# First product and gelu of 64 of 128 expert tiles computed beside the top-k routing and kept in device memory

## What is computed

```python
def _peer(x, w_q, sub_keys, u_tab, v_tab):
    q = (xt @ w_q).reshape(T, PEER_HEADS, 2, PEER_DK // 2)
    s = jnp.einsum('thpd,hpkd->thpk', q, sub_keys)
    s1, i1 = lax.top_k(s[:, :, 0], PEER_TOPK)
    s2, i2 = lax.top_k(s[:, :, 1], PEER_TOPK)
    cand_s = s1[..., :, None] + s2[..., None, :]          # all pairs
    top_s, pos = lax.top_k(cand_s, PEER_TOPK)
    gate = jax.nn.softmax(top_s, axis=-1)
    hid = jnp.einsum('td,thkd->thk', xb, u_tab[ib])       # first product
    coef = jax.nn.gelu(hid, approximate=False) * gb
    return jnp.einsum('thk,thkd->td', coef, v_tab[ib])    # second product
```

## Time and profile before

| | us |
|---|---|
| median of 3 runs (2864.67 to 2868.19) | 2864.67 |
| the profiled execution | 2865.48 |
| its span in the trace | 2863.7 |
| of it `peer_route` (DVE's first to last operation) | 107.7 |
| of it `peer_table` | 107.4 |
| of it the expert stream, first matmul to last | 721.4 |

### The profile page before, as it was taken

The page is one execution under the profiler, slowest core; times in us unless marked ns, Lnnn a source line. Parts: engine busy times, 40 slices in busy tenths (PEclk is TensorE's granted clock), DMA queues, the critical chain, the costliest instruction groups (busy, mean ns, idle before and its releaser), DMA issues. The chain is left out here.

```text
span 2863.7 us, 43489 instructions
## 1 busy us (share of the span) xinstructions
PE 2196.3 (77%) x16766; PEld 1930.6 (67%) x16766; DVE 1775.3 (62%) x2988; ACT 903.8 (32%) x1244; POOL 113.3 (4%) x102
## 2 busy tenths in 40 slices
PE   4936665997844599679778876550679999999997
PEld 2936334996733599467476776550569999999996
DVE  2564226776775677467336668459976666666665
ACT  1300222432323233132322422220554444444443
POOL 0000000000000000043000023000000000000000
PEclk8955557999865799889765988785899999999998
DMA  5635005884702487231100000310025555555554
GB/s 184 221 59 151 0 2 183 320 310 171 258 10 76 160 299 281 74 119 59 59 3 1 5 3 27 138 59 0 0 95 185 183 189 190 184 183 190 189 183 148
DMA packets 153588, 368.84 MB, mean 129 GB/s; under 512 B 10992, under 2 KB 93680, under 8 KB 141296
## 3 DMA queue, kind: packets, MB, share of 16 engines
q1 hardware_dynamic: 153312, 365.93, 36.7%
q10 hardware_dynamic: 144, 1.05, 0.1%
HBM read 364.32 MB, written 2.62 MB: 128 GB/s over the span
## 5 line engine op out<-in xcount | busy, mean ns | idle before, releaser
L981 PE MATMUL experts_pa<-all_h_hi,experts_u_hi 128*128 128x256 f32 x1024 | 290.1, 283 | 7.4 <-DVE experts_u_lo L1052 7.4
L983 PE MATMUL experts_pa<-all_h_hi,experts_u_lo 128*128 128x256 f32 x1024 | 290.5, 284 | 0.0
L982 PE MATMUL experts_pa<-all_h_lo,experts_u_hi 128*128 128x256 f32 x1024 | 290.5, 284 | 0.0
L1228 PE MATMUL ffn_pa<-all_h_hi,ffn_u_hi 128*128 128x256 f32 x704 | 198.6, 282 | 29.6 <-DVE ffn_u_lo L1287 29.6
L1057 DVE TENSOR_TENSOR experts_v_lo<-experts_v,experts_v_hi 128x1024 fp32r<-128x1024 f32 x128 | 156.8, 1225 | 92.1 <-ACT experts_v_hi L1026 92.1
L981 PEld LDWEIGHTS experts_pa<-all_h_hi,experts_u_hi 128*128 128x128 f32 x1024 | 196.9, 192 | 12.5 <-DVE experts_u_lo L1052 7.6
L994 PE MATMUL experts_py<-experts_v_lo,experts_c_hi 128*128 128x512 f32 x512 | 201.0, 393 | 0.0
L982 PEld LDWEIGHTS experts_pa<-all_h_lo,experts_u_hi 128*128 128x128 f32 x1024 | 196.9, 192 | 4.9
L993 PE MATMUL experts_py<-experts_v_hi,experts_c_hi 128*128 128x512 f32 x512 | 200.1, 391 | 0.0
L1229 PE MATMUL ffn_pa<-all_h_lo,ffn_u_hi 128*128 128x256 f32 x704 | 198.1, 281 | 0.0
L1230 PE MATMUL ffn_pa<-all_h_hi,ffn_u_lo 128*128 128x256 f32 x704 | 197.9, 281 | 0.0
(11 more groups left out here) (543 smaller groups left out, 5467.5 us busy)
## 6 DMA issues: line engine op xcount, KB each, us to landing
experts_u<-in_peer_u SPq DMA_DIRECT2D x128, 512.0 KB, 4.4
experts_v<-in_peer_v SPq DMA_DIRECT2D x128, 512.0 KB, 3.3
ffn_u<-in_ffn_columns SPq DMA_DIRECT2D x44, 1024.0 KB, 7.9
ffn_ada_w<-in_ada_w SPq DMA_DIRECT2D x36, 1024.0 KB, 5.4
ffn_v<-in_ffn_rows SPq DMA_DIRECT2D x44, 512.0 KB, 8.1
proj_ada_w<-in_ada_w SPq DMA_DIRECT2D x12, 1024.0 KB, 5.7
proj_w<-in_diff_w_in SPq DMA_DIRECT2D x12, 1024.0 KB, 5.8
main_mod<-in_dn_w_qkv SPq DMA_DIRECT2D x24, 512.0 KB, 3.3
```

What stands on the lines that cost most here:

```text
L981: pe.matmul(out, u_hi[:, b, cols], h_hi[:, c, :], start=(c == 0), stop=False)
L982: pe.matmul(out, u_hi[:, b, cols], h_lo[:, c, :], start=False, stop=False)
L983: last = pe.matmul(out, u_lo[:, b, cols], h_hi[:, c, :], start=False, stop=(c == KT - 1))
L1228: pe.matmul(out, u_hi[:, b, cols], h_hi[:, c, :], start=(c == 0), stop=False)
```

## The change

`peer_route` gets a second job beside the routing: for tiles 0 to 63 it loads `u` (a ring of three buffers), splits it, multiplies it, applies gelu, and SP stores the result `hid` (128 x 256, 128 KB a tile) to a tensor `hid_kept` in device memory. On VectorE, `low_u` (the subtraction of one tile) is put between the groups of the top-16 search and of the `hot` steps. ScalarE does `high_u` two tiles ahead of the gelu; one `Exp` per token block stands between. SP's list holds loads and stores in turn. TensorE has the 64 products ahead of the six transposes.

`streamed_mlp` is replaced by `experts`, which is written out for all 128 tiles. For tiles 0 to 63 it loads `hid` (a ring of three) and `v`, and does only the weighing and `down`. For tiles 64 to 127 it does what was done before.

```diff
+        u = st.sb("u", [P, ring, D])
+        u_hi, u_lo = (st.sb(n, [P, ring, D], F32R) for n in ("u_hi", "u_lo"))
+        hid = st.sb("hid", [P, ring, S])
...
+        @block.sync
+        def _(sp):
+            for i in range(early + 2):
+                if i < early:
+                    if i >= ring:
+                        sp.wait_ge(u_split, i - ring + 1)
+                    sp.dma_start(u[:, i % ring, :], ins["peer_u"][i]).then_inc(u_loaded[i % ring], 16)
+                if i >= 2:
+                    sp.wait_ge(acted, i - 1)
+                    sp.dma_start(hid_kept[i - 2], hid[:, (i - 2) % ring, :]).then_inc(hid_kept_done[(i - 2) % ring], 16)
...
+            def low_u():
+                nonlocal tiles
+                if tiles < early:
+                    b = tiles % ring
+                    dve.wait_ge(u_hi_ready, tiles + 1)
+                    dve.tensor_tensor(u_lo[:, b, :], u[:, b, :], u_hi[:, b, :].bitcast(F32), ALU.subtract
+                                      ).then_inc(u_split, 1)
+                    tiles += 1
...
                 first = [done.at(dve.max(out_v[:, 0:8], values)) for values, out_v, _ in lists]
+                low_u()
...
                     rest.append(done.at(dve.match_replace(spare[n], out_v[:, 0:8], values, NEG)))
+                low_u()
...
                     second.append(done.at(dve.max(out_v[:, 8:16], spare[n])))
+                low_u()
...
+                    if n == 1 and values.shape[-1] > P:
+                        low_u()
+                low_u()
...
+            def high_u(i):
+                act.wait_ge(u_loaded[i % ring], 16 * (i // ring + 1))
+                if i >= ring:
+                    act.wait_ge(rows_ready, i - ring + 1)
+                act.copy(u_hi[:, i % ring, :], u[:, i % ring, :]).then_inc(u_hi_ready, 1)
+
+            def gate_tile(i):
+                act.wait_ge(rows_ready, i + 1)
+                if i >= ring:
+                    act.wait_ge(hid_kept_done[i % ring], 16 * (i // ring))
+                act.activation(hid[:, i % ring, :], pa[:, i % 2, 0:S], ACT.Gelu).then_inc(acted, 1)
+
+            high_u(0)
+            high_u(1)
+            for i in range(early):
+                if i + 2 < early:
+                    high_u(i + 2)
...
+                gate_tile(i)
...
+            for i in range(early):
+                b = i % ring
+                pe.wait_ge(u_split, i + 1)
+                if i >= 2:
+                    pe.wait_ge(acted, i - 1)
```

The stream in the changed kernel:

```diff
+            for i in range(n_tiles):
+                if i < early:
+                    if i >= ring:
+                        sp.wait_ge(weighed, i - ring + 1)
+                    sp.dma_start(hid[:, i % ring, :], hid_kept[i]).then_inc(hid_loaded[i % ring], 16)
+                if i >= 2:
                     sp.wait_ge(v_split, i - 1)
...
+                sp.dma_start(v[:, i % 2, :], rows[i]).then_inc(v_loaded[i % 2], 16)
+                j = i + 1 - early
+                if 0 <= j < late:
+                    if j >= 2:
+                        sp.wait_ge(u_split, j - 1)
+                    sp.dma_start(u[:, j % 2, :], columns[i + 1]).then_inc(u_loaded[j % 2], 16)
...
+            for i in range(n_tiles + 1):
+                if early <= i < n_tiles:
+                    up(i - early)
+                if i >= 1:
+                    down(i - 1)
...
+            high_v(0)
+            for i in range(n_tiles):
+                if i >= early:
+                    gate_tile(i - early)
+                if 0 <= i + 2 - early < late:
+                    high_u(i + 2 - early)
+                if i + 1 < n_tiles:
+                    high_v(i + 1)
...
+            low_v(0)
+            for i in range(n_tiles):
+                weigh(i)
+                if 0 <= i + 2 - early < late:
+                    low_u(i + 2 - early)
+                if i + 1 < n_tiles:
+                    low_v(i + 1)
```

More of the change, by code:

```diff
@@ L967, in _, with up @@
+            sp.wait_ge(u_split, late)
+            sp.dma_start(x, kept[0]).then_inc(x_loaded, 16)
             sp.wait_ge(v_split, n_tiles)
-            sp.dma_start(gate, kept[1]).then_inc(kept_loaded, 16)
+            sp.dma_start(gate, kept[1]).then_inc(gate_loaded, 16)
         @block.tensor
         def _(pe):
[L972 to L983, removed]
+            def up(j):
+                b = j % 2
+                pe.wait_ge(u_split, j + 1)
+                if j >= 2:
+                    pe.wait_ge(acted, j - 1)
+                out = pa[:, b, 0:S]
+                for c in range(KT):
+                    cols = slice(c * P, (c + 1) * P)
+                    pe.matmul(out, u_hi[:, b, cols], h_hi[:, c, :], start=(c == 0), stop=False)
+                    pe.matmul(out, u_hi[:, b, cols], h_lo[:, c, :], start=False, stop=False)
+                    last = pe.matmul(out, u_lo[:, b, cols], h_hi[:, c, :], start=False, stop=(c == KT - 1))
@@ L984, in up, with down @@
                 last.then_inc(rows_ready, 1)
-            def down(i, b, start=False, stop=False):
+            def down(i):
+                b = i % 2
+                start, stop = i == 0, i == n_tiles - 1
                 pe.wait_ge(coef_ready, i + 1)
@@ L1028, in gate_tile @@
[L1028 to L1058, removed]
+            def high_u(j):
+                act.wait_ge(u_loaded[j % 2], 16 * (j // 2 + 1))
+                if j >= 2:
+                    act.wait_ge(rows_ready, j - 1)
+                act.copy(u_hi[:, j % 2, :], u[:, j % 2, :]).then_inc(u_hi_ready, 1)
+            def high_v(i):
+                act.wait_ge(v_loaded[i % 2], 16 * (i // 2 + 1))
+                if i >= 2:
+                    act.wait_ge(down_done, i - 1)
+                act.copy(v_hi[:, i % 2, :], v[:, i % 2, :]).then_inc(v_hi_ready, 1)
@@ new lines, in low_v, with weigh @@
+            def low_v(i):
+                dve.wait_ge(v_hi_ready, i + 1)
+                dve.tensor_tensor(v_lo[:, i % 2, :], v[:, i % 2, :], v_hi[:, i % 2, :].bitcast(F32), ALU.subtract
+                                  ).then_inc(v_split, 1)
+            def weigh(i):
+                b = i % 2
+                if i < early:
+                    dve.wait_ge(hid_loaded[i % ring], 16 * (i // ring + 1))
+                    rows_of = hid[:, i % ring, :]
+                else:
+                    dve.wait_ge(acted, i - early + 1)
+                    rows_of = act_out[:, (i - early) % 2, :]
+                dve.tensor_tensor(coef[:], rows_of, table[:, i, :], ALU.mult).then_inc(weighed, 1)
```

134 lines of the change are left out of this document (63 added, 71 removed).

## The result

| | us |
|---|---|
| before, median of 4 runs beside the changed kernel | 2866.16 (2864.67 to 2868.19) |
| changed, median of 4 runs | 2971.60 (2969.18 to 2975.23) |
| ratio, 95% interval | 1.0368 [1.0350, 1.0386] |
| predicted | 2963, range 2920 to 3025 |
| span of the changed kernel's profiled execution | 2973.5 |

The change makes the kernel 3.7% slower. The busy time by stretch is read first again; it answers the earlier trace rows. The stretches are the routing, the first 64 tiles of the stream, the rest of it, and ten microseconds within the first 64. Columns: start:end, length, busy us and instructions of each engine, granted clock (PEclk), DMA share, GB/s.

The account below looks back on a forecast made before the run. It took VectorE to bound the routing and TensorE the stream before; after, one load in flight would pace the routing. 2865.48 + 242 - 144 = 2963.5, less 0.8 for the median: 2963 us, range 2920 to 3025.

Parts of the forecast that it names:

- The ring: Routing: load, rounding, gelu and store wait on each other, one load in flight; 5.4 us a tile, stage +242 us.
- The start and the end: Routing: fourth load issued at 12.2 us; after the last subtraction, 7.8 us remain to the last copy.
- The two `Exp` fall into waits: Routing, ScalarE: both operations fit into its waiting time, adding nothing to the 350 us stage.
- TensorE in the routing: Routing: busy half of the time; even a half-clock `up` of 5.1 us stays under 5.4 and costs nothing.
- The stream: First 64 tiles at 3.3 us each, the rest at 5.62; 583.5 us in place of 727.4, -144.
- The cold stream: Rival, 3%: TensorE at half clock in the stream's first 64 tiles, 5.3 us a tile, +128, total 3091 us.
- the joint: Stream, where tile 64 begins: `u(0)` loaded one tile late for ScalarE, 1 to 4 us, 3 taken.
- the lead: Stream start: first issue to first matmul takes 7.6 us, 6.0 before.
- Loads that run ahead: Rival, 6%: in the routing SP does not stand still at the stores; stage 201 us, total 2814 us.
- Later landings: Rival, 9%: in the routing store and load share the queue's rings; 6.3 to 6.6 us a round, 3017 to 3035.
- gain and cost would cancel: Rival, 1%: no change to be seen in the total, needing a routing round of 3.8 us.

Follow-up runs that it names:

- gelu first: Changed kernel with ScalarE doing the gelu of tile i ahead of the rounding of tile i+2, SP's list untouched: 2847.5 us (one run).
- 96 early tiles: Changed kernel with stores four tiles back, weighing ahead of `v_lo`, three `v` buffers, and 96 tiles moved in place of 64: 2784.23 us, 0.9721 of before.
- lag of four: Changed kernel with SP storing the `hid` of tile i-4 (in place of i-2) behind the load of tile i, five `hid` buffers: 2812.61 us, 0.9812 of before.

## Why the prediction held

**The ring.** It was the step that decided, and it held in detail: a round of 5.4 us, made of a landing of 3.67 (3.6 taken), 0.95 (0.94), 0.41 (0.42) and 0.37. Over all: the fourth load is issued at 1917.57, the 64th at 2249.57, 332.0 / 60 = 5.53; without the two long rounds, (332.0 - 6.0) / 60 = 5.43.

**The start and the end.** The fourth load was predicted 12.2 us after the stage's first issue and came after 13.2. The first rows of ScalarE and TensorE show where:

```profile
1908.91 1.04 ACT L2532 CAST route_u_hi<-route_u 128x1024 fp32r<-128x1024 f32 x1 [4.80 <-DMA route_u<-in_peer_u]
...
1911.27 0.58 PE L2561 MATMUL route_pa<-all_h_hi,route_u_hi 128*128 128x256 f32 x1 [7.78 <-DVE route_u_lo L2453]
...
1916.79 0.39 ACT L2538 ACTIVATE route_hid<-route_pa 128x256 f32<-128x256 f32 x1 [3.04 <-PE route_pa L2563]
```

The first load took 4.55 us from its issue at 1904.36 (3.65 in the earlier trace rows). Here three loads were issued together, but that alone doesn't explain it: ten of the runs above start with the same three loads, and in them the first rounding comes between 3.2 us (gelu first) and 4.7 (96 early tiles) after the first issue. What else sets it stays open. The rest was as worked out: 2.36 to the first matmul, then 5.52 for the `up` at half clock to its gelu and 0.78 to the next load, for 5.1 and 1.1. From the last load to the last copy it is 13.3, 13.8 predicted.

**The step that failed** is the sentence "The two `Exp` fall into waits". I counted the 1.9 us that ScalarE was busy in the routing before, one table load among them, and took it that an engine with 255 us of waits has room. But its waits are the ring's landings. The `Exp` stands between the rounding and the gelu, where ScalarE has no wait at all, and it brings two table loads with it, since gelu and `Exp` alternate: 1.28 + 0.31 + 1.28 and the small gaps make 3.0 us, twice 6.0. The stage: 350 predicted + 6.0 + 1.0 at the start + 60 x 0.03 - 0.5 at the end = 358.3 of 358.5. In an engine that waits, an operation behind the wait lengthens the round by all of its time; only ahead of the wait could the idle time cover it. An `Exp` ahead of the rounding wasn't run. In every row here the table load for the gelu stands right ahead of the gelu, so part of the 3.0 us might remain even then.

**TensorE in the routing.** I took it to be busy half of the time; it was for 244 of 358 us, since at a granted clock of 0.84 on average an `up` took 244 / 64 = 3.8 us. That it costs nothing was right: 3.8 is under 5.4, and with a lag of four, at 0.98, the same products took 188 us.

**The stream.** 3.3 us a tile predicted, 3.33 in the steady rhythm, 215.1 / 63 = 3.41 overall. The difference is in three places: the half-clock start (the first two tiles took 8.18 in place of 6.67), two pairs longer by 0.4 to 0.5, and one disturbance. The steady pair is 6.67 where the pieces gave 6.47: 0.12 is the start of TensorE behind the gap, which the prediction had put at "a little" and rounded up for. In the disturbance a `v` landed 5.7 us after its issue, and ScalarE waited for it:

```profile
2524.66 1.05 ACT L1011 CAST experts_v_hi<-experts_v 128x1024 fp32r<-128x1024 f32 x1 [4.30 <-DMA experts_v<-in_peer_v]
```

The granted clock of that stretch was 0.87:

```profile
2520.00:2533.00 13.00, 10.57 (x39) 8.22 (x40) 6.88 (x13) 2.73 (x4) 0.00 (x0) 0.87 0.61 200
```

That cost 2.8 us. The cold stream that was a rival is this row, for 13 us rather than for all of the 215; in the rest, but for the start, the clock was 1.00, with TensorE busy for 86% of the time (117.2 of the 136 us from 2380 to 2516). The gap of 0.9 in each pair rather than 0.5 in each tile is the same time. At the joint nothing was lost: the first `up`, at 2592.91, follows the `down` ahead of it without a gap, where 3 us had been taken. That and the longer first 64 tiles nearly cancel, which is luck: 583.5 predicted for the stream, 585.2 measured. The half with `up` in it is 362.6 = 64 x 5.62 + 2.74, and the lead was 7.5 us for 7.6.

**What cancelled and what didn't.** The stream came 1.7 us above its sum and the routing 8.5. The profiled execution took 2975.23 us where the sum gave 2963.5: 11.7 apart, 8.5 of it in the routing, 1.7 in the stream, 1.2 outside of both. It is the `Exp` and the first landing for the most part. The median, 2971.6, is 8.6 above the 2963 predicted for it; the profiled execution was the longest of the four, so some of its 11.7 is its own.

**The rivals.** Loads that run ahead would have given 2814 by the sum of that paragraph; the lag of four, which makes them do it, gave 2812.6. So its arithmetic was right (201 us of routing for 199.9), and its condition wasn't met. The Trainium skill, page Perfetto Trace Analysis, section DMA Optimizations, says that it may make sense to give inputs and outputs an issuing engine each. The runs agree in part: the mixed list is one half of what cost the time, ScalarE's order the other (gelu first, 124 us less with SP's list untouched). And one queue with both in it, the stores asked for late enough, reaches the time at which TensorE is the bound. Stores on a second queue weren't tried here, so whether that would do as well is open. Later landings (6.3 us a round and more) didn't come: the 128 KB ahead made 0.3 of a landing, as had been scaled. Seven single rounds took 6.1 to 6.3 us, besides the two with an `Exp`. The mean of the rounds never came near the 3.8 at which gain and cost would cancel.

## What to carry to other kernels

Buffers don't tell how many transfers are in flight: follow a load through the engines' lists (landing, first use, what stands behind that, who waits for it, what that one issues next), and if the path comes back to the next load, the round is the sum of all of it. Where it does, first try what takes one link out of it: here the store of an older tile, or the gelu ahead of the next rounding. Each engine's total waits point at another engine, so they don't show the ring; only all lists together do. And of an operation put into an engine with much idle time, look at which side of the wait it stands.

## What the runs showed of the hardware

- A table load of 1.28 us stands at each change between gelu and `Exp` on ScalarE: one `Exp` of 0.31 us between two gelus lengthened its round by 3.0 us.
- Of 128 KB of store issued right ahead of a 512 KB load, the load's landing shows 0.3 us (3.6 against 3.3 median), the issue 0.37. Loads at 2.88 us apart rather than 5.4 landed 0.2 later.
- TensorE, busy for 68% of the routing with a gap of 1.8 us in a round (104.1 us in 59 times), had a granted clock of 0.84 on average; in the stream, busy for 86% with a gap of 0.9 in every 6.7 us, it had 1.00, but for its first tiles and the one stretch above.
- A `down` that starts behind a gap of 0.9 us takes 2.86 us to the next one's start, one in full flow 2.74.
